# How the first layer's input is squared, split and first used: ScalarE's row sums, units ahead of the norm, norm weights over another queue

## The reference, cut to what matters

```
def _rmsnorm(x, g):
    xf = x.astype(jnp.float32)
    y = xf * lax.rsqrt(jnp.mean(xf * xf, axis=-1, keepdims=True) + EPS)
    return (y * g.astype(jnp.float32)).astype(x.dtype)
...
    for i in range(DEPTH):
        xn = _rmsnorm(x, W['norm_mix_g'][i])
        z = jnp.einsum('bld,dk->blk', xn, W['w_in'][i])
```

## Time and profile before

| | us |
|---|---|
| median of 3 runs (5221.86 to 5233.71) | 5227.57 |
| the profiled execution, its own time | 5225.91 |
| its span, first to last instruction | 5224.3 |
| PE busy | 4976.5 (95%) |
| DVE busy | 3403.5 (65%) |
| ACT busy | 1596.9 (31%) |
| POOL busy | 401.8 (8%) |
| mean granted TensorE clock | 0.974 of full speed |

### The profile page before, as it was taken

One profiled execution on the slowest core, in us unless ns is written; L12 is line 12 of the kernel. 1 busy time (PEld: TensorE's weight loads), 2 busy tenths in 40 slices (PEclk: granted clock), 3 DMA queues, 4 the chain that ended last, 5 costly groups with the idle time before them and its releaser, 6 DMA issues.

```text
span 5224.3 us, 86720 instructions
## 1 busy us (share of the span) xinstructions
PE 4976.5 (95%) x33128; PEld 4899.1 (94%) x33129; DVE 3403.5 (65%) x5297; ACT 1596.9 (31%) x2280; POOL 401.8 (8%) x246
## 2 busy tenths in 40 slices
PE   8999999999998999999959999999999999999979
PEld 7999999999998999999949999999999999999968
DVE  5677756444556756866557777666668777866665
ACT  2112122111113311122224444333334444443333
POOL 3111101110102021110010000000000000000020
PEclk8999999999999999999979999999999999999979
DMA  3111111111111111111035554444445555644431
GB/s 95 50 37 40 49 39 41 41 48 40 48 41 43 40 55 47 39 40 42 27 133 181 172 172 161 151 145 151 153 148 196 180 189 175 199 166 156 145 122 41
DMA packets 398929, 527.54 MB, mean 101 GB/s; under 512 B 12056, under 2 KB 353606, under 8 KB 398616
## 3 DMA queue, kind: packets, MB, share of 16 engines
q1 hardware_dynamic: 359552, 460.75, 26.8%
q0 software_dynamic: 11136, 33.97, 1.9%
q10 hardware_dynamic: 27928, 28.60, 1.6%
HBM read 494.87 MB, written 28.39 MB: 100 GB/s over the span
## 4 chain that ended last, share of the span: by engine, by line
PE 50%; issue 6%; DVE 5%; DMA 1%; ACT 1%; DVEq 0%; ACTq 0%; SPq 0%
PE PS L661 11%; PE PS L662 11%; PE PS L663 11%; PE PS L765 4%; PE PS L766 4%; PE PS L767 4%; DMA WRAW<-in_moe_w_gate 1%; DVE WLO L1519 1%; DVE YB L1850 1%; PE PS L718 1%; PE PS L719 1%; PE PS L720 1%; DVE EACC L2246 1%; DVE XSL L2195 1%; PE PS L960 0%
## 5 line engine op out<-in xcount | busy, mean ns | idle before, releaser
L1519 DVE TENSOR_TENSOR WLO<-WRAW,WHI 128x1024 fp32r<-128x1024 f32 x866 | 1065.2, 1231 | 330.9 <-ACT WHI L1136 203.6
L661 PE MATMUL PS<-XHI,WHI 128*128 128x384 f32 (+1 forms) x3648 | 1202.4, 330 | 1.5 <-DVE XLO L1746 1.2
L663 PE MATMUL PS<-XHI,WLO 128*128 128x384 f32 (+1 forms) x3648 | 1197.5, 328 | 0.0
L662 PE MATMUL PS<-XLO,WHI 128*128 128x384 f32 (+1 forms) x3648 | 1197.0, 328 | 0.0
L1136 ACT ACTIVATE WHI<-WRAW 128x1024 fp32r<-128x1024 f32 x866 | 898.9, 1051 | 948.1 <-PE PS L767 662.1
L661 PE MATMUL PS<-XSH,WHI 128*128 128x232 f32 (+6 forms) x3584 | 1061.9, 296 | 36.6 <-issue 19.2
L662 PE MATMUL PS<-XSL,WHI 128*128 128x232 f32 (+6 forms) x3584 | 1057.8, 295 | 0.0
L663 PE MATMUL PS<-XSH,WLO 128*128 128x232 f32 (+6 forms) x3584 | 1057.0, 295 | 0.0
L661 PEld LDWEIGHTS PS<-XSH,WHI 128*128 128x128 f32 x3584 | 682.5, 190 | 40.1 <-issue 32.8
L661 PEld LDWEIGHTS PS<-XHI,WHI 128*128 128x128 f32 x3648 | 691.0, 189 | 4.0 <-DVE XLO L1746 2.4
L662 PEld LDWEIGHTS PS<-XLO,WHI 128*128 128x128 f32 x3648 | 690.8, 189 | 0.7
(11 more groups left out here) (367 smaller groups left out, 5767.5 us busy)
## 6 DMA issues: line engine op xcount, KB each, us to landing
WRAW<-in_moe_w_gate SPq DMA_DIRECT2D x112, 1024.0 KB, 5.0
WRAW<-in_moe_w_up SPq DMA_DIRECT2D x112, 1024.0 KB, 5.0
WRAW<-in_moe_w_down SPq DMA_DIRECT2D x112, 1024.0 KB, 4.9
WRAW<-in_w_in SPq DMA_DIRECT2D x48, 1024.0 KB, 5.2
WRAW<-in_ffn_w_gate SPq DMA_DIRECT2D x11, 1024.0 KB, 5.3
WRAW<-in_ffn_w_up SPq DMA_DIRECT2D x11, 1024.0 KB, 5.3
WRAW<-in_ffn_w_down SPq DMA_DIRECT2D x11, 1024.0 KB, 4.9
XG<-sorted_rows POOLq DMA_DIRECT2D x18, 512.0 KB, 4.5
```

Of the source, the lines that this page charges most:

```text
L661: pe.matmul(PS[:, bank, 0:n], wh, hi(k), start=(k == 0), stop=False)
L662: pe.matmul(PS[:, bank, 0:n], wh, lo(k), start=False, stop=False)
L663: ins = pe.matmul(PS[:, bank, 0:n], wl, hi(k), start=False, stop=(k == KC - 1))
L1519: v.do(dve.tensor_tensor(WLO[s][:], raw_view(conv.n // 2 % RAW, conv.n % 2, kind), WHI[s][:].bitcast(F32), ALU.subtract), conv)
```

## The change

Five edits, all in the start of layer 0.

1. The seven DMAs of the norm gains (NRS) move from POOL's queue to ACT's, as the first things that ACT does, with a semaphore of their own (`nrs_loaded`). PE transposes NRS ahead of everything else, and DVE copies it to PAR and releases the folds (`par_ready`) before the first chunk of `x`. The other parameters keep their place after block 1.
2. ACT no longer squares each transposed chunk, and DVE no longer adds squares: for each of the 24 chunks ACT makes the copy XHI and DVE the difference XLO, with no temporary between them.
3. The squares are instead taken from XIN as it was loaded (tokens on partitions): nine ACT instructions of 128 x 1024 (the last of 64 x 1024) that overwrite XIN with its squares and accumulate their sum along the row into RTOK. They stand after ACT's first two weight conversions. DVE waits for all nine (`norm_rows`), then asks for the square root as before.
4. PE drops `stats()` in layer 0; the first column unit follows the last transpose directly, and `spread()` stands after the first block of the second unit.
5. Of the three weight conversions ahead of the norm, the third moves behind the squares on ACT and behind the diagonals on DVE.

```diff
@@ POOL
-        for j in range(7):
-            src = (A["norm_mix_g"][j % 2] if j < 2 else A["norm_ffn_g"][j % 2] if j < 4 else A["norm_ple_g"][j % 2] if j < 6
-                   else A["final_norm_g"])
-            g.dma_start(NRS[j * KC:(j + 1) * KC, :], src.rearrange("(k p) -> k p", p=P)).then_inc(S["par_loaded"], 16)
@@ PE
         pe.wait_ge(S["consts"], 3)
+        pe.wait_ge(S["nrs_loaded"], 16 * 7)
+        b = misc_bank()
+        pe.transpose(PS[:, b, 0:7 * KC], NRS[:], IDF[0:7 * KC, 0:7 * KC]).then_inc(m.next(), 1)
         for block, (t0, n) in enumerate(BLOCKS):
...
-            stats()
-            column_unit(XHI, XLO, first_use=(W_MIX1 if l else None))
-            spread()
-            column_unit(XHI, XLO)
+            if l:
+                stats()
+                column_unit(XHI, XLO, first_use=W_MIX1)
+                spread()
+                column_unit(XHI, XLO)
+            else:
+                use()
+                slot = unit.n % HL
+                for j, (t0, n) in enumerate(BLOCKS):
+                    pe.wait_ge(S["evicted"], KC * (j + 1))
+                    b = open_bank()
+                    product(b, n, slot, lambda k: XHI[:, k, t0:t0 + n], lambda k: XLO[:, k, t0:t0 + n]).then_inc(q.next(), 1)
+                unit.n += 1
+                column_unit(XHI, XLO, after_first=spread)
@@ ACT
-        act.wait_ge(S["consts"], 3)
+        for j in range(7):
+            src = (A["norm_mix_g"][j % 2] if j < 2 else A["norm_ffn_g"][j % 2] if j < 4 else A["norm_ple_g"][j % 2] if j < 6
+                   else A["final_norm_g"])
+            act.dma_start(NRS[j * KC:(j + 1) * KC, :], src.rearrange("(k p) -> k p", p=P)).then_inc(S["nrs_loaded"], 16)
         for t0, n in BLOCKS:
             for c in range(KC):
                 act.wait_ge(S["mm_done"], q.n + 1)
-                src = PS[:, q.n % BANKS, 0:n]
-                act.activation(XHI[:, c, t0:t0 + n], src, ACT.Copy)
-                if split.n >= 2:
-                    act.wait_ge(S["split_done"], split.n - 1)
-                act.activation(T[2 + split.n % 2][:, 0:n], src, ACT.Square).then_inc(split.next(), 1)
+                act.activation(XHI[:, c, t0:t0 + n], PS[:, q.n % BANKS, 0:n], ACT.Copy).then_inc(split.next(), 1)
                 q.n += 1
-        m.n += 1
-        for _ in range(LOOK):
-            convert()
+        m.n += 2
+        convert()
+        convert()
+        act.wait_ge(S["rtok_clear"], 1)
+        for block, (t0, n) in enumerate(BLOCKS):
+            tiles = range(t0 // P, -(-(t0 + n) // P))
+            act.wait_ge(S[f"x_loaded{block}"], 16 * len(tiles))
+            for j in tiles:
+                w = tokens(j)
+                act.activation(XIN[0:w, j, :], XIN[0:w, j, :], ACT.Square, accum_out=RTOK[0:w, j:j + 1]).then_inc(S["row_squares"], 1)
+        convert()
@@ DVE
+        def norm_rows():
+            dve.wait_ge(S["row_squares"], NT)
+            request()
+            v.do(dve.reciprocal(RTOK[:], RTOK[:]))
+            v.sync()
...
                 v.do(dve.tensor_tensor(XLO[:, c, t0:t0 + n], ps[:, 0:n], XHF[:, c, t0:t0 + n], ALU.subtract), q)
-                sq = T[2 + split.n % 2][:, 0:n]
-                if c == 0:
-                    v.do(dve.tensor_copy(SQS[:, t0:t0 + n], sq), split)
-                else:
-                    v.do(dve.tensor_tensor(SQS[:, t0:t0 + n], SQS[:, t0:t0 + n], sq, ALU.add), split)
-                v.sync()
...
-            norm()
+                norm()
+            else:
+                norm_rows()
+                diagonals()
+                convert()
+                spread_rstd()
```

More of the change, by code:

```diff
@@ L783, in _ @@
             if block == 1:
-                pe.wait_ge(S["par_loaded"], 16 * (7 + 12))
+                pe.wait_ge(S["par_loaded"], 16 * 12)
                 b = misc_bank()
@@ L787, in _ @@
                     for c in range(2):
-                        pe.transpose(PS[:, b, (l * 2 + c) * 38:(l * 2 + c) * 38 + 38], PRS[:, l, c * P:(c + 1) * P], IDF[0:38, 0:38])
-                pe.transpose(PS[:, b, 152:152 + 7 * KC], NRS[:], IDF[0:7 * KC, 0:7 * KC]).then_inc(m.next(), 1)
+                        ins = pe.transpose(PS[:, b, (l * 2 + c) * 38:(l * 2 + c) * 38 + 38], PRS[:, l, c * P:(c + 1) * P], IDF[0:38, 0:38])
+                ins.then_inc(m.next(), 1)
         for l in range(DEPTH):
-            stats()
-            column_unit(XHI, XLO, first_use=(W_MIX1 if l else None))
-            spread()
-            column_unit(XHI, XLO)
+            if l:
[12 more added lines that the diff above has]
+                column_unit(XHI, XLO, after_first=spread)
             use(2)
@@ L1225, in _ @@
             plain(2)
-            m.n += 1
+            m.n += 1 if l else 0
             convert()
@@ L1717, in _ @@
         v.do(dve.memset(RTOK[:], 1.0))
+        v.sync()
+        dve.sem_inc(S["rtok_clear"], 1)
+        ps = misc_ready()
+        v.do(dve.tensor_copy(PAR[:, 152:152 + 7 * KC], ps[:, 0:7 * KC]), m)
+        v.sync()
+        dve.sem_inc(S["par_ready"], 1)
         for j, (t0, n) in enumerate(BLOCKS):
@@ L1721, in _ @@
                 ps = main_ready()
-                dve.wait_ge(S["split_hi"], split.n + 1)
+                dve.wait_ge(S["split_hi"], sreq.n + 1)
                 sreq.n += 1
                 v.do(dve.tensor_tensor(XLO[:, c, t0:t0 + n], ps[:, 0:n], XHF[:, c, t0:t0 + n], ALU.subtract), q)
-                sq = T[2 + split.n % 2][:, 0:n]
-                if c == 0:
-                    v.do(dve.tensor_copy(SQS[:, t0:t0 + n], sq), split)
-                else:
-                    v.do(dve.tensor_tensor(SQS[:, t0:t0 + n], SQS[:, t0:t0 + n], sq, ALU.add), split)
-                v.sync()
             if j == 1:
                 ps = misc_ready()
-                v.do(dve.tensor_copy(PAR[:], ps[:, 0:4 * 38 + 7 * KC]), m)
-                v.sync()
-                dve.sem_inc(S["par_ready"], 1)
+                v.do(dve.tensor_copy(PAR[:, 0:152], ps[:, 0:152]), m)
+        v.sync()
+        split.n += sreq.n
+        dve.sem_inc(S["split_done"], sreq.n)
         dve.sem_inc(S["split_req"], sreq.n)
-        dve.sem_inc(sqc.next(), 1)
-        for _ in range(LOOK):
-            convert()
+        convert()
+        convert()
         for l in range(DEPTH):
```

3 lines of the change are left out of this document (2 added, 1 removed).

## The result

The changed kernel takes 5196.30 us (median of 5 runs, 5192.43 to 5199.55) against 5227.57 us before: ratio 0.9940, 95% interval 0.9925 to 0.9954. That is 31.3 us gained where 15.6 were forecast, and it lies outside the predicted range.

The account below looks back on a forecast made before the run. PE, busy 95% of the span, was taken to bound the kernel, so only its idle start could be won: first product at 31.5 instead of 45.62. 5225.91 - 14.1 = 5211.8, given as 5212 us, range 5202 to 5222.

Parts of the forecast that it names:

- What bounds the start: Start-up: data wait, DVE's pace, a collision of some 6 us, token sums; afterwards x_sample sets block 2 at 20.9 us.
- The clock in block 2: Block 2's transposes on PE: half clock, 8 x 0.96 = 7.7 us, ending at 28.7.
- clock held: Rival, PE's start: gapless transposes from 9 to 20 keep full clock; gain 16.5 to 18.9 us, 5207 to 5209; 20%.
- First product: PE's start: first product at 31.5 us against 45.62 before, 14.1 us gained.
- Both are done by 25.0 at the latest.: POOL's first two weight folds, 3.6 us each: tile 1 lands by 21.4 us, PAR is ready at about 10.
- The first two units: PE from first product to V: first unit again 14.2 us, total work unchanged, V groups at 59.6 instead of 73.72.
- Squares: Nine row squares on ACT: 1.05 us each, 9.4 in all, ending at 40.5; diagonals at about 46, no cost.
- norm late: Rival, ahead of the spread: squares cost twice a copy, diagonals at 55.6; gain 8.4 us, 5217.5; 15%.
- gains late: Rival, PE's start: gain DMAs stall on ACT and land at 30.8; first product at about 52, 5232 us; 4%.
- The V collision: Tile 3's fold at 60 to 63.5 across DVE's sixth WLO, ahead of the first V eviction: charged 0, at most 1 us.
- likeliest case: Whole kernel: gain 11 to 16 us, own range 5206 to 5218 with the runs' scatter; 58%.
- the sum's last sentence: Behind the start-up: nothing later depends on absolute time, as weight loads wait for conversions and these for PE; no further gain.

Follow-up runs that it names:

- e12: The changed kernel with 256 idle instructions on PE, 140 ahead of its first transpose and 116 ahead of its first product: 5220.01 us (ratio 0.9983).
- e6: The changed kernel with 16 idle instructions on PE ahead of its first transpose: 5206.09 us (ratio 0.9952).
- e14: The changed kernel with 16 idle instructions on PE behind the last expert item: 5193.60 us (ratio 0.9932).
- e7: The changed kernel with 25 idle instructions on DVE alone in the start-up: 5201.49 us (ratio 0.9940).

## Why the prediction was right in the start and wrong in size

**What bounds the start.** Right. x_sample set block 2 (20.39, forecast 20.9), and POOL's fold, DVE's sums and the token sums left the path.

**The clock in block 2.** Half, as chosen: 24 transposes in 7.38 us (forecast 7.7). They did not bring the clock back, though PE was busy without a gap from 22 to 26. The rival "clock held" did not occur, and neither did its condition, transposes without a gap from 9 to 20: blocks 0 and 1 ran at full clock and were through at 16.8 (20 to 21.5 forecast), PE then waited 3.17 us for x_sample, and the clock fell in that wait. e12 has transposes without a gap by accident, since its idle instructions hold PE until x_sample is there. Its transposes run from 22.82 without a wait, and block 2's take 4.64 us in place of 7.38:

```profile
31.46 4.64 PE L782 MATMUL PS<-IDF,XIN 128*128 128x128 f32 x24
```

The stretch of e12 with most of them, at a granted clock of 1.00:

```profile
32.00:34.00 2.00, 2.00 (x12) 1.21 (x11) 2.00 (x6) 1.51 (x5) 2.00 (x5) 1.00 0.42 121
```

**First product.** 30.50 against 31.5: x_sample 0.5 early, transposes 0.3 and hand-overs 0.2 shorter.

**"Both are done by 25.0 at the latest."** Wrong, without harm. The second fold waited for tile 1's load (forecast for 21.4 at the latest), not for PAR, and ran from 23.07 to 26.67; the first weight copy came at 28.14, so 1.5 us of cover were left. POOL's rows answer to the earlier trace rows:

```profile
15.48 3.60 POOL L546 TENSOR_TENSOR WRAW<-WRAW,PAR 128x2048 f32<-128x2048 f32 x1 [7.11 <-DMA WRAW<-in_w_in]
23.07 3.60 POOL L546 TENSOR_TENSOR WRAW<-WRAW,PAR 128x2048 f32<-128x2048 f32 x1 [3.98 <-DMA WRAW<-in_w_in]
...
58.17 3.61 POOL L546 TENSOR_TENSOR WRAW<-WRAW,PAR 128x2048 f32<-128x2048 f32 x1 [15.37 <-DMA WRAW<-in_w_in]
```

**The first two units.** From first product to V 27.25 us against 28.10 before: the clock rose sooner. I had kept them equal, 0.85 us too dear.

**Squares.** 1.04 us each against the 1.05 chosen; "norm late" did not occur: the spread stood 1.9 us sooner than forecast and still did not wait. The gain rows landed at 8.97 (forecast 9.5), "gains late" did not occur.

**The V collision.** Foreseen in place and price: fold 58.17 to 61.78, and DVE's WLO stretched across it, with the first V eviction right behind (62.78, inside the cover).

```profile
59.11 3.75 DVE L1535 TENSOR_TENSOR WLO<-WRAW,WHI 128x1024 fp32r<-128x1024 f32 x1 [0.66 <-ACT WHI L1145]
62.78 0.47 DVE L1792 TENSOR_SCALAR V<-PS,RTOK 128x256 f32<-128x256 f32 x1
```

**The chances.** They do not add up. The likeliest case (0.58) and "clock held" (0.20) give at most 0.78 for "faster by more", where 0.83 is written, and "within" should be 0.18 or more.

**The step that failed** is the sum's last sentence: "Nothing later depends on absolute time: weight loads wait for conversions, and these for PE." With it the sum put the rest at nothing. It holds for data and not for code. Removing instructions from the start moved every later instruction in its engine's program, and with it the code of the expert items that PE jumps to. Of the 31.3 us, 16.0 are the start-up (14.1 forecast) and 15.3 the rest (0 forecast). In the profiled executions all of the rest lies in the items, 21.2 us, less 3.6 given back behind them. The items take 2244.6 us on average over the seven kernels at place 0, 2254.5 over the five at 16 and 18, and 2263.0 over the four at 34 and 35. What is shown is that the place of PE's item code moves the rest (e6 against e14 and e12). That its 34 instructions are the whole of the 15.3 us is the best reading of the table, but no run moves the changed kernel by 34. DVE's place may have a share of its own: e7 puts it at 3.5 to 6.9 us by the medians, but its one stage time (2250.2, against 2247.8 in e12) does not set it apart from scatter. That PE's later place is now a good one is luck of the change, not its merit.

## What to carry to other kernels

In a program with branches, a change's effect is its own work plus where it leaves the code behind it. Before crediting or blaming a change of a few tenths of a per cent, run it with a handful of idle instructions ahead of the loop and again behind it. Count what a change takes out in the trace and not in the source: here each matmul came with a weight load that takes a place of its own. In the trace, a product released by "issue" right behind a jump, with an instruction block landing up to 1 us ahead of it, is a sign of this stall. It is not the whole of its price, so compare the whole stage between kernels, and set each kernel against one measured beside it.

## What was not expected of the hardware

- Sixteen idle instructions ahead of the branches cost 6 to 11 us in 5196; 256 cost the same stages 1.6 us or nothing.
- At a jump PE stood still for 3 us behind its data, until half a microsecond after an instruction block had landed, and half clock lasted another 5.
- 256 idle instructions on PE lengthened the start-up by 22 us. The 116 ahead of the first product held PE for 16.10 us, 0.14 us each, and the 140 ahead of the first transpose moved it from 8.97 to 22.57, although they overlap the wait for data.
- Transposes of float32 without a gap did not bring the clock back from half in 4 us (22 to 26), but kept it at full from 22.8 to 36 in e12; products brought it back 3 to 5 us after they began.
